# A two-layer decoder trunk: table loads moved ahead of stores, gate stores in quarters, and the dots of a V slot moved ahead of its split

## The chip, the cores and the metric

The kernel runs on one core of a Trainium2 chip. The metric is the device time of one execution in microseconds. The median of three timed runs before the change is 3729.75 us (3727.84 to 3729.91).

## The reference, cut to what matters

The reference is one inference step of a two-layer decoder. After a mixer each layer has an expert-retrieval block, and the change touches only this block:

```python
def _peer(x, wq, keys, u_tab, v_tab):
    q = (xf @ wq).reshape(n, PEER_HEADS, 2, PEER_DK // 2)
    s = jnp.einsum('nhpd,hpkd->nhpk', q, keys)
    ...                                   # top 16 of 128, twice; top 16 of the 256 sums: experts, gate
    def one(args):
        xi, ei, gi = args
        hi = jax.nn.gelu(jnp.einsum('bed,bd->be', jnp.take(u_tab, ei, axis=0), xi))
        return jnp.einsum('be,bed->bd', gi * hi, jnp.take(v_tab, ei, axis=0))
```

There are 520 tokens, 8 heads of 16 experts each, and two tables of 16,384 rows of 1024 numbers in each layer.

## The kernel before

**Two ways for the tokens.** For 392 tokens the whole tables are multiplied on TensorE ("dense"). The other 128 tokens gather their 128 rows of each table by indirect DMA on GpSimd, and VectorE takes the products ("dots", 256 a layer: 128 with U, 128 with V).

**Stage U.** The table U comes in 128 chunks of 512 KB. Chunk c goes through a ring of RING = 4 places: SyncE (SP) loads it into `wraw` (`load_chunk`, L509), ScalarE rounds it to `whi` (`round_chunk`, L673), VectorE writes the rest to `wlo` (`split_chunk`, L941), TensorE multiplies it in 24 matmuls (`first_table`, L1626), and ScalarE takes the product through a gelu into `hid` (`take_hidden`, L806). SP then stores `hid` to DRAM (`store_h`, L535). The first eight chunks are mixed with 16 chunks of the query weights (`mixed`, L104). The ring is closed by semaphores: a load of chunk s+4 waits for `w_lo` of chunk s, and the rounding of chunk s+4 waits until TensorE is done with chunk s.

**Gates.** From chunk 28 on, TensorE also builds the dense gate matrix, 98 groups of four tokens (`gate_group`, L1659), one group behind each chunk up to chunk 115 and two behind each of 116 to 120. VectorE and ScalarE write the one-hot operands `oh` of a group one chunk ahead (`one_hots`). ScalarE copies the result to `gst` (`take_gates`, L854). Seven groups make a block of 1792 KB; `gst` holds two blocks, and SP stores a block to DRAM in one DMA (`store_gates`, L540), two chunks after its last group. `take_gates` waits at the first group of a block until the block two before it has been stored.

**The loop on SP** (L558 to L565), one step for each chunk, in this order: `load_next(slot)`, which issues the load four chunks on, then `store_h` of the chunk in this slot, which waits until ScalarE has taken it, then a gate store if one is due. SP runs its program in order, so a load stands behind the store of the chunk before.

**VectorE in U**, one step for each chunk from 8 on (L1217 to L1224): split, one-hots, a part of the ranking of experts (`RANK_BY`), then dots of the sparse tokens, which begin at chunk 77: 105 dots before stage U ends. ScalarE in U, in order: take the product, round the chunk four on, one-hots, take the gates.

**Stage V.** The gates come back from DRAM (`gc`), also the hidden values (`hl`); VectorE multiplies them to `wt` (`gated`), ScalarE rounds that to `wth`, VectorE writes the rest to `wtl` (`split_wt`), and TensorE multiplies with the 128 chunks of V, 24 matmuls each (`second_table`, L1701). VectorE's step c is written out at L1246 to L1252: `gated(c + 3)`, `split_wt(c + 2)`, `split_next` (the split of the chunk four on), `dots(N_U + c)`. Every fifth step has two dots, the others one. ScalarE's step c (L912 to L916): round `wt` of c+3, then round the chunk c+4, which waits until TensorE is done with chunk c.

**Gathers.** GpSimd fills five row buffers; the gather of dot n waits until dot n-5 is done (L645).

Of the kernel before, what the change touches and what calls it, by code (L numbers as in the profile page):

```python
# [30 lines left out]
P = 128  # L31
# [30 lines left out]
BLOCK = SPAN_T // SUB  # L62
NB = ND // SPAN_T
# [12 lines left out]
N_AB, N_WO, N_WQ, N_U, N_INC = 24, 8, 16, 128, 16  # L76
# [3 lines left out]
C_MIX = [C_WO0 + N_WO, 0]  # L80
# [23 lines left out]
def mixed(slot):  # L104

    if slot >= N_MIX:
        return "u", slot - N_WQ
    return ("u", slot // 3) if slot % 3 == 2 else ("q", slot // 3 * 2 + slot % 3)


def groups_by(c):

    return min(N_GROUPS, max(0, min(c, G_TWO) - G_ONE) + 2 * max(0, min(c, G_END) - G_TWO))


def group_slot(n):

    return next(c for c in range(N_U) if groups_by(c + 1) > n)


LOOK = 1
CHUNK_NS, GROUP_NS, SPLIT_NS, HOTS_NS, DOT_NS = 4300, 890, 1300, 1550, 1250
RANK_NS = [1900] + [480] * 4 + [650] * 4 + [630] * 4 + [480] * 4 + [650] * 3 + [4400] + [2350] * 6 + [1300]
EXP_PART = 20
# [2 lines left out]
def plan():  # L127
# [5 lines left out]
    for c in range(MIXED, N_U):  # L133
        hots = groups_by(c + 1 + LOOK) - groups_by(c + LOOK)
        room += CHUNK_NS + GROUP_NS * (groups_by(c + 1) - groups_by(c)) - SPLIT_NS - HOTS_NS * hots
# [109 lines left out]
def trunk(nc, i, o):  # L245
    with ExitStack() as ctx:
# [94 lines left out]
        gst = place("gst", [P, 2, P, SPAN_T], F32)  # L341
# [23 lines left out]
        gates = [nc.dram_tensor(f"gates{n}", (NB, P, P, SPAN_T), F32, kind="Internal").ap() for n in range(DEPTH)]  # L365
# [6 lines left out]
        def sem(name):  # L372
            return ctx.enter_context(nc.semaphore(name))
# [16 lines left out]
        gates_out = [sem(f"gates_out{n}") for n in range(2)]  # L390
# [113 lines left out]
        @block.sync  # L504
        def _(e):
            for dst, src in ((xt[:], i["xt"]), (wf[:], i["wf"]), (vec[:], i["vec"]), (cst[:], i["cst"])):
                e.dma_start(dst, src).then_inc(setup_in, 16)

            def load_chunk(s, src):  # L509

                if s >= RING:
                    e.wait_ge(w_lo, s - RING + 1)
                e.dma_start(wraw[:, s % RING, :], src).then_inc(w_in[s % RING], 16)

            def chunk_source(s):

                for layer in range(DEPTH):
                    if C_V[layer] <= s < C_V[layer] + N_U:
                        at = (layer * N_U + s - C_V[layer]) * P
                        return i["v"][at:at + P, :]  # L520
                    if C_MIX[layer] <= s < C_V[layer]:
                        kind, n = mixed(s - C_MIX[layer])
                        if kind == "u":
                            return i["u"][layer * N_U + n].rearrange("p k c -> p (k c)")
                        s = C_MIX[layer] + n
                        break
                return i["w"][s - (2 * N_U if s > C_V[0] else 0)].rearrange("p k c -> p (k c)")

            def load_next(s):
                if s + RING < N_CHUNKS:  # L530
                    load_chunk(s + RING, chunk_source(s + RING))

            def peer_tables(layer):

                def store_h(c):  # L535

                    e.wait_ge(chunk_taken, taken(C_MIX[layer]) + table_at(c) + 1)
                    e.dma_start(hidden[layer][c], hid[:, c % RING, :]).then_inc(h_out[c % RING], 16)

                def store_gates(b):  # L540

                    e.wait_ge(gate_taken, layer * N_GROUPS + (b + 1) * BLOCK)
                    e.dma_start(gates[layer][b], gst[:, b % 2]).then_inc(gates_out[b % 2], 16)

                def load_h(c):
                    if c >= RING:
                        e.wait_ge(g_used, layer * N_U + c - RING + 1)
                    e.wait_ge(h_out[c % RING], 16 * (layer * N_U // RING + c // RING + 1))
                    e.dma_start(hl[:, c % RING, :], hidden[layer][c]).then_inc(h_in[c % RING], 16)

                def load_gates(g, half):
                    if g >= 2 and half == 0:
                        e.wait_ge(g_used, layer * N_U + CPL * (g - 1))
                    at = slice(half * (NB // 2), (half + 1) * (NB // 2))
                    e.dma_start(gc[:, g % 2, at].rearrange("p b c n -> p b (c n)"),
                                gates[layer][at, :, g * CPL:(g + 1) * CPL, :].rearrange("b p c n -> p b (c n)")).then_inc(g_in[g % 2], 16)

                for slot in range(N_WQ + N_U):  # L558
                    load_next(C_MIX[layer] + slot)
                    kind, c = mixed(slot)  # L560
                    if kind == "u":
                        store_h(c)
                        for b in range(NB):
                            if c == group_slot((b + 1) * BLOCK - 1) + 2:
                                store_gates(b)  # L565
                for par in range(2):
                    e.wait_ge(gates_out[par], 16 * (NB // 2) * (layer + 1))
                load_gates(0, 0)
                load_gates(0, 1)
                for c in range(RING):  # L570
                    load_h(c)
                for c in range(N_U):
                    load_next(C_V[layer] + c)
                    if c + RING < N_U:
                        load_h(c + RING)
                    if c % CPL < 2 and c // CPL + 1 < N_U // CPL:
                        load_gates(c // CPL + 1, c % CPL)

            for s in range(RING):
                load_chunk(s, chunk_source(s))  # L580
            for s in range(N_AB - 2):
                load_next(s)
            e.wait_ge(pages_in, 16)
            e.wait_ge(chunk_done, C_WO0)
            load_cached(e, 0, 0, i["ck"], None)
            load_cache(e, 0)

            e.wait_ge(pv_done, HEADS * QT)
            for s in range(N_AB - 2, C_MIX[0]):
                load_next(s)  # L590
            peer_tables(0)
            for s in range(C_INC, C_MIX[1]):
                load_next(s)
            peer_tables(1)
            for k in range(KB):
                e.wait_ge(ln_out, 8 * 4 + k + 1)
                e.dma_start(o["y"][:, k, :], xt[:, k, :]).then_inc(y_out, 16)
            e.wait_ge(y_out, 16 * KB)
# [73 lines left out]
        def _(e):  # L672
# [123 lines left out]
            def peer(layer):  # L796
# [57 lines left out]
                def take_gates(n):  # L854

                    b = n // BLOCK
                    if n % BLOCK == 0 and (b >= 2 or layer):
                        e.wait_ge(gates_out[b % 2], 16 * (layer * (NB // 2) + b // 2))
                    e.wait_ge(gate_done, layer * N_GROUPS + n + 1)
                    e.activation(gst[:, b % 2, :, n % BLOCK * SUB:(n % BLOCK + 1) * SUB],  # L860
                                 aux[:, n % 2, :].rearrange("p (a n) -> p a n", n=SUB), ACT.Copy).then_inc(gate_taken, 1)
# [18 lines left out]
                for slot in range(N_WQ + N_U):  # L880
                    kind, n = mixed(slot)
# [14 lines left out]
                    if kind == "u":  # L896
                        for g in range(groups_by(n + LOOK), groups_by(n + 1 + LOOK)):
                            one_hots(g)
# [39 lines left out]
        def _(e):  # L938
# [7 lines left out]
            def split_next(s):  # L946
                if s + RING < N_CHUNKS and not C_AB + N_AB - 2 <= s < C_AB + N_AB:
                    split_chunk(s + RING)
# [207 lines left out]
            def peer(layer):  # L1156
# [37 lines left out]
                def dots(slot):  # L1194

                    for n in range(dots_by(slot - 1), dots_by(slot)):
                        dot(n)
# [19 lines left out]
                for n in range(MIXED, N_U):  # L1217
                    split_next(C_MIX[layer] + table_at(n))
                    for g in range(groups_by(n + LOOK), groups_by(n + 1 + LOOK)):
                        one_hots(g)  # L1220
# [16 lines left out]
                def split_wt(c):  # L1237
                    e.wait_ge(wt_hi, layer * N_U + c + 1)
                    e.tensor_tensor(wtl[:, c % RING, :], wt[:, c % 2, :], wth[:, c % RING, :].bitcast(F32), ALU.subtract).then_inc(wt_lo, 1)  # L1239
# [6 lines left out]
                for c in range(N_U):  # L1246
                    if c + 3 < N_U:
                        gated(c + 3)
                    if c + 2 < N_U:
                        split_wt(c + 2)  # L1250
                    split_next(C_V[layer] + c)
                    dots(N_U + c)  # L1252

                e.wait_ge(dot_done, (layer + 1) * DOTS)
                e.tensor_tensor(ysum[0:ST, 0, :], ysum[0:ST, 0, :], ysum[0:ST, 1, :], ALU.add).then_inc(y_ready, 1)
# [610 lines left out]
```

## Time and profile before

| what | value |
|---|---|
| median of three runs | 3729.75 us |
| profiled execution | 3736.83 us, of it a span of 3734.8 us |
| TensorE busy | 91% of the span |
| VectorE, ScalarE, GpSimd busy | 66%, 39%, 21% |
| moved by DMA | 835 MB, 224 GB/s over the span |

The profiled execution is 7.1 us (0.2%) above the median. Stage U of the first layer lies between 491 and 1333 us of the span, V between 1354 and 1949; in the second layer they lie between 2246 and 3088 and between 3109 and 3703. Matmul records overlap, so TensorE's busy share says little; the distance of one chunk's end to the next is what counts.

### The profile page before, as it was taken

The page shows a single profiled execution, that of the slowest core. Times are in us where ns is not written, and L with a number is a line of the kernel's source. Part 1 is how long each engine was busy: PE and PEld are TensorE (multiplying, and loading weights), DVE is VectorE, ACT ScalarE, POOL GpSimd, SP SyncE. Part 2 cuts the span into 40 slices and gives each one's busy share as a digit, 9 for nine tenths or more (in the row PEclk, how much of TensorE's full clock was granted, in tenths as well). Part 3 has the DMA queues.
Part 4 walks back from the last instruction along what each step waited for, and adds up shares of the span by engine and source line. Part 5 has one row for each costly group of instructions (what it writes and reads, how often), then busy time and mean ns, then how long its engine had stood idle before and what let it go on. Part 6 is the DMA issues. An engine that isn't in the chain of part 4 may idle for free.

```text
span 3734.8 us, 54628 instructions
## 1 busy us (share of the span) xinstructions
PE 3397.7 (91%) x19630; PEld 3154.9 (84%) x19630; DVE 2474.6 (66%) x5134; ACT 1444.4 (39%) x2581; POOL 767.2 (21%) x690
## 2 busy tenths in 40 slices
PE   8998999999988979999988889999998897999998
PEld 8833789999988969998988789999888887989897
DVE  3243379777666767777773348876776666777777
ACT  3222143455545523333323223345554552333333
POOL 3211010000143332222221000000023333222221
PEclk9898999999999989999999789999999998999999
DMA  4354313454688899999971112355468889999994
GB/s 138 118 150 124 127 68 110 157 187 164 219 306 303 282 370 331 339 325 337 324 266 59 35 51 90 123 176 182 158 241 297 298 315 351 341 325 340 323 337 160
DMA packets 315827, 835.34 MB, mean 224 GB/s; under 512 B 32249, under 2 KB 155257, under 8 KB 311441
## 3 DMA queue, kind: packets, MB, share of 16 engines
q1 hardware_dynamic: 233472, 541.63, 42.6%
q0 software_dynamic: 82192, 291.85, 22.3%
q8 instruction: 66, 1.08, 0.1%
q14 instruction: 97, 0.79, 0.1%
HBM read 726.25 MB, written 107.11 MB: 223 GB/s over the span
## 4 chain that ended last, share of the span: by engine, by line
PE 51%; DVE 17%; DMA 11%; issue 10%; ACT 10%; SPq 1%; DVEq 0%; ACTq 0%; POOLq 0%; POOL 0%
PE pstr L1632 20%; PE pstr L1421 13%; DMA wraw<-in_u 8%; DVE ysum L1192 8%; ACT whi L678 7%; PE aux L1667 4%; DVE wt L1233 3%; PE aux L1709 2%; PE pstr L1709 2%; PE pstr L1543 2%; PE pstr L1563 1%; DVE wlo L944 1%; DVE rows L1179 1%; DMA wraw<-in_v 1%; PE aux L1452 1%
## 5 line engine op out<-in xcount | busy, mean ns | idle before, releaser
L944 DVE TENSOR_TENSOR wlo<-wraw,whi 128x1024 fp32r<-128x1024 f32 x600 | 733.8, 1224 | 868.4 <-ACT whi L678 867.7
L678 ACT ACTIVATE whi<-wraw 128x1024 fp32r<-128x1024 f32 x600 | 629.3, 1050 | 341.0 <-DMA wraw<-in_u 212.6
L1632 PE MATMUL pstr<-xh,whi 128*128 128x392 f32 x2048 | 734.5, 359 | 5.3 <-ACT hid L812 5.3
L1632 PE MATMUL pstr<-xl,whi 128*128 128x392 f32 x2048 | 711.3, 347 | 0.0
L1632 PE MATMUL pstr<-xh,wlo 128*128 128x392 f32 x2048 | 709.0, 346 | 0.0
L651 POOL DMA_INDIRECT rows<-in_ur,idx x256 | 343.8, 1343 | 1532.0 <-DVE hs L1179 962.3
L1709 PE MATMUL aux<-wth,whi 128*128 128x392 f32 x1024 | 373.1, 364 | 97.9 <-DVE wtl L1239 97.1
L908 ACT ACTIVATE wth<-wt 128x392 fp32r<-128x392 f32 x256 | 136.1, 532 | 823.4 <-DVE wt L1233 823.4
L651 POOL DMA_INDIRECT rows<-in_v,idx x256 | 290.7, 1136 | 712.3 <-DVE ysum L1192 627.0
L1632 PEld LDWEIGHTS pstr<-xh,whi 128*128 128x128 f32 x2048 | 398.3, 194 | 6.0 <-issue 5.9
L1632 PEld LDWEIGHTS pstr<-xl,whi 128*128 128x128 f32 x2048 | 397.1, 194 | 0.0
L1632 PEld LDWEIGHTS pstr<-xh,wlo 128*128 128x128 f32 x2048 | 395.7, 193 | 0.0
L1709 PE MATMUL aux<-wth,wlo 128*128 128x392 f32 x1024 | 351.1, 343 | 0.0
L1709 PE MATMUL pstr<-wth,wlo 128*128 128x392 f32 x1024 | 350.1, 342 | 0.0
L1709 PE MATMUL aux<-wtl,whi 128*128 128x392 f32 x1024 | 350.1, 342 | 0.0
L1709 PE MATMUL pstr<-wtl,whi 128*128 128x392 f32 x1024 | 348.7, 341 | 0.0
L1709 PE MATMUL pstr<-wth,whi 128*128 128x392 f32 x1024 | 347.6, 340 | 0.0
L1667 PE MATMUL aux<-oh,oh 128*128 128x128 f32 x1568 | 227.3, 293 | 115.1 <-DVE oh L1212 114.6
L1667 PEld LDWEIGHTS aux<-oh,oh 128*128 128x128 f32 x1568 | 213.3, 204 | 131.7 <-issue 67.2
L1709 PEld LDWEIGHTS aux<-wth,whi 128*128 128x128 f32 x1024 | 193.0, 188 | 150.0 <-DVE wtl L1239 97.4
L1421 PE MATMUL pstr<-xh,whi 128*128 128x260 f32 x1408 | 295.4, 291 | 26.1 <-DVE xl L959 25.8
L1192 DVE SCALAR_TENSOR_TENSOR ysum<-rows,hs,ysum 128x1024 f32<-128x1024 f32 x252 | 318.7, 1278 | 0.5
(240 smaller groups left out, 5405.9 us busy)
## 6 DMA issues: line engine op xcount, KB each, us to landing
wraw<-in_u SPq DMA_DIRECT2D x256, 512.0 KB, 4.4
wraw<-in_v SPq DMA_DIRECT2D x256, 512.0 KB, 4.9
hidden<-hid SPq DMA_DIRECT2D x256, 196.0 KB, 1.9
gates<-gst SPq DMA_DIRECT2D x28, 1792.0 KB, 8.6
gc<-gates SPq DMA_DIRECT2D x64, 784.0 KB, 8.6
hl<-hidden SPq DMA_DIRECT2D x256, 196.0 KB, 5.3
wraw<-in_w SPq DMA_DIRECT2D x88, 512.0 KB, 3.5
kv<-in_ck SPq DMA_DIRECT2D x32, 256.0 KB, 3.2
```

Of the source, the lines that this page charges most:

```text
L651: e.indirect_dma_start(rows[0:ST, n % BUFS, :], None, table, bass.IndirectOffsetOnAxis(ap=idx[0:ST, j:j + 1], axis=0)).then_inc(rows_in[n ...
L678: e.activation(whi[:, s % RING, :], wraw[:, s % RING, :], ACT.Copy).then_inc(w_hi, 1)
L908: e.activation(wth[:, c % RING, :], wt[:, c % 2, :], ACT.Copy).then_inc(wt_hi, 1)
L944: e.tensor_tensor(wlo[:, s % RING, :], wraw[:, s % RING, :], whi[:, s % RING, :].bitcast(F32), ALU.subtract).then_inc(w_lo, 1)
L1179: e.tensor_tensor_reduce(data, data, xrow[0:ST, :], 1.0, 0.0, ALU.mult, ALU.add, hs[0:ST, 0, j:j + 1]).then_inc(dot_done, 1)
L1192: e.scalar_tensor_tensor(y, data, w, y, ALU.mult, ALU.add).then_inc(dot_done, 1)
L1233: e.tensor_tensor(wt[:, n % 2, :].rearrange("p (b n) -> p b n", n=SPAN_T), hl[:, n % RING, :].rearrange("p (b n) -> p b n", n=SPAN_T), gc[ ...
L1421: mm = e.matmul(pstr[:, r % 2, h, 0:HALF], w[:, r, k * P:(k + 1) * P], x[:, k, h * HALF:(h + 1) * HALF], start=k == 0 and w is whi and x i ...
L1543: mm = e.matmul(cached[0:BH, half, :].rearrange("p (g c) -> p g c", g=4), qd[:, b, k, :], pages[:, :, k * P:(k + 1) * P], start=False, sto ...
L1632: mm = e.matmul(pstr[:, r % 2, 0, 0:ND], w[:, r, k * P:(k + 1) * P], x[:, k, 0:ND], start=k == 0 and w is whi and x is xh, stop=k == KB - ...
L1667: mm = e.matmul(out[:, :, r], oh2[:, slot, r, :], oh1[:, slot, r, :], start=True, stop=True)
L1709: mm = e.matmul(bank(d)[:, 0:ND], w[:, r, d * P:(d + 1) * P], x[:, r, :], start=first and w is whi and x is wth, stop=last and w is wlo)
```

## The change

It does three things. First, the loop on SP runs three steps longer, and the stores in a step belong to the slot three before it: the load of chunk s+4 is now issued after the store of chunk s-4 and not after that of chunk s-1. Second, a gate block leaves in four DMAs of 448 KB, each with a quarter of `gst`'s middle axis; the first leaves with the store of the chunk after the block's last group, the others with the three stores that follow. The semaphore counts go up by the factor PIECES. Third, in VectorE's step of stage V the dots stand ahead of the split.

```diff
+BEHIND, PIECES = 3, 4
...
-                def store_gates(b):
+                def store_gates(b, part):
 
                     e.wait_ge(gate_taken, layer * N_GROUPS + (b + 1) * BLOCK)
-                    e.dma_start(gates[layer][b], gst[:, b % 2]).then_inc(gates_out[b % 2], 16)
+                    at = slice(part * (P // PIECES), (part + 1) * (P // PIECES))
+                    e.dma_start(gates[layer][b][:, at, :], gst[:, b % 2, at, :]).then_inc(gates_out[b % 2], 16)
...
-                for slot in range(N_WQ + N_U):
-                    load_next(C_MIX[layer] + slot)
-                    kind, c = mixed(slot)
+                for slot in range(N_WQ + N_U + BEHIND):
+                    if slot < N_WQ + N_U:
+                        load_next(C_MIX[layer] + slot)
+                    kind, c = mixed(slot - BEHIND) if slot >= BEHIND else ("q", 0)
                     if kind == "u":
                         store_h(c)
                         for b in range(NB):
-                            if c == group_slot((b + 1) * BLOCK - 1) + 2:
-                                store_gates(b)
+                            for part in range(PIECES):
+                                if c == min(group_slot((b + 1) * BLOCK - 1) + 1 + part, N_U - 1):
+                                    store_gates(b, part)
                 for par in range(2):
-                    e.wait_ge(gates_out[par], 16 * (NB // 2) * (layer + 1))
+                    e.wait_ge(gates_out[par], 16 * PIECES * (NB // 2) * (layer + 1))
...
-                        e.wait_ge(gates_out[b % 2], 16 * (layer * (NB // 2) + b // 2))
+                        e.wait_ge(gates_out[b % 2], 16 * PIECES * (layer * (NB // 2) + b // 2))
...
                         split_wt(c + 2)
+                    dots(N_U + c)
                     split_next(C_V[layer] + c)
-                    dots(N_U + c)
```

SP around the first gate block of the first layer, before: a load (`wraw`), the store of the chunk in the same slot (`hidden`), and the whole block behind the store of one chunk.

```order
L513 DMA wraw<-in_u 128x1024
L538 DMA hidden<-hid 128x392
L513 DMA wraw<-in_u 128x1024
L538 DMA hidden<-hid 128x392
L543 DMA gates<-gst 128x3584
L513 DMA wraw<-in_u 128x1024
L538 DMA hidden<-hid 128x392
L513 DMA wraw<-in_u 128x1024
```

The same place on SP now; a `hidden` row belongs to the chunk three before the one whose slot it stands in.

```order
L514 DMA wraw<-in_u 128x1024
L539 DMA hidden<-hid 128x392
L545 DMA gates<-gst 128x896
L514 DMA wraw<-in_u 128x1024
L539 DMA hidden<-hid 128x392
L545 DMA gates<-gst 128x896
L514 DMA wraw<-in_u 128x1024
L539 DMA hidden<-hid 128x392
L545 DMA gates<-gst 128x896
L514 DMA wraw<-in_u 128x1024
L539 DMA hidden<-hid 128x392
L545 DMA gates<-gst 128x896
```

What moved: the gate block is in four pieces with a load between each two, and every load stands three stores nearer to the program's start.

VectorE early in stage V of the first layer, before: `wlo` is the split, the two L1179 rows are one dot.

```order
L1233 TENSOR_TENSOR wt<-hl,gc 128x392
L1239 TENSOR_TENSOR wtl<-wt,wth 128x392
L944 TENSOR_TENSOR wlo<-wraw,whi 128x1024
L1179 ISA rows,hs<-rows,xrow 128x1024
L1179 ISA hs 128x1
L1233 TENSOR_TENSOR wt<-hl,gc 128x392
```

The same place on VectorE now.

```order
L1237 TENSOR_TENSOR wt<-hl,gc 128x392
L1243 TENSOR_TENSOR wtl<-wt,wth 128x392
L1183 ISA rows,hs<-rows,xrow 128x1024
L1183 ISA hs 128x1
L948 TENSOR_TENSOR wlo<-wraw,whi 128x1024
L1237 TENSOR_TENSOR wt<-hl,gc 128x392
```

What moved: the dot stood between the split and the next chunk's `wt`, and now stands ahead of the split, so that `wt` of the next chunk follows the split at once.

## Rows read from the trace of the kernel before

**Rows 1.** Timeline by engine around a gate store (start us, us, instruction, [idle <-releaser]):

```profile
891.84 0.43 SPq L543 DMA_DIRECT2D gates<-gst  x1
892.31 0.46 SPq L513 DMA_DIRECT2D wraw<-in_u  x1
...
900.01 1.06 ACT L678 ACTIVATE whi<-wraw 128x1024 fp32r<-128x1024 f32 x1 [3.38 <-DMA wraw<-in_u]
...
903.75 1.84 PE L1667 MATMUL aux<-oh,oh 128*128 128x128 f32 x8 [2.48 <-DVE oh L1212]
906.63 0.74 PE L1656 MATMUL aux<-cst,dense_pick 96*128 96x96 f32 x3 [1.04 <-DVE dense_pick L1378]
```

**Rows 2.** Chain of waits, pieces in order of time (start us, us, what):

```profile
629.10 25.76 PE pstr L1632 x144
...
729.73 0.89 PE aux L1667 x8
```

**Rows 3.** Timeline of SP: stores of chunks 28, 77, 116 and 127, first layer:

```profile
723.01 0.33 SPq L538 DMA_DIRECT2D hidden<-hid  x1
...
1012.54 0.32 SPq L538 DMA_DIRECT2D hidden<-hid  x1
...
1269.49 0.32 SPq L538 DMA_DIRECT2D hidden<-hid  x1
...
1333.21 0.32 SPq L538 DMA_DIRECT2D hidden<-hid  x1
```

**Rows 4.** Stretches: length, busy of PE, PEld, DVE, ACT, POOL; PEclk, DMA share, GB/s:

```profile
490.00:630.00 140.00, 140.00 (x1088) 139.91 (x1086) 118.56 (x612) 48.85 (x82) 1.81 (x2) 1.00 0.26 92
723.00:1012.50 289.50, 268.23 (x1574) 263.93 (x1574) 205.70 (x484) 167.35 (x355) 15.34 (x11) 0.96 0.53 179
1012.50:1269.50 257.00, 220.21 (x1258) 216.11 (x1259) 175.32 (x306) 128.91 (x284) 102.07 (x73) 0.93 0.86 304
1269.50:1354.50 85.00, 57.35 (x340) 56.75 (x339) 55.32 (x92) 33.91 (x69) 33.99 (x26) 0.86 0.90 336
1354.50:1900.00 545.50, 523.76 (x2821) 500.23 (x2822) 416.89 (x519) 172.60 (x235) 154.43 (x137) 1.00 0.95 332
```

**Rows 5.** Waits, 720 to 1355 us, PE (for whom: us, times, longest):

```profile
PE aux L1667 <- DVE oh L1212: 57.4, 21, 6.2
```

**Rows 6.** Waits of SP's queue, 630 to 1310 us:

```profile
SPq L538 <- ACT hid L812: 566.7, 116, 9.8
SPq L513 <- DVE wlo L944: 1.7, 1, 1.7
```

**Rows 7.** DMA issues of the whole span: KB each, median us to landing:

```profile
wraw<-in_u SPq DMA_DIRECT2D x256, 512.0 KB, 4.4
gates<-gst SPq DMA_DIRECT2D x28, 1792.0 KB, 8.6
rows<-in_ur,idx POOLq DMA_INDIRECT x256, 6.9
```

**Rows 8.** Timeline of ACT and DVE over one slot of stage V:

```profile
1365.11 1.04 ACT L678 ACTIVATE whi<-wraw 128x1024 fp32r<-128x1024 f32 x1
...
1366.18 1.23 DVE L944 TENSOR_TENSOR wlo<-wraw,whi 128x1024 fp32r<-128x1024 f32 x1 [1.07 <-ACT whi L678]
1367.33 1.22 DVE L1179 CUSTOM_DVE_ANT_0 rows<-rows,xrow 128x1024 f32<-128x1024 f32 x1
...
1368.47 0.56 DVE L1233 TENSOR_TENSOR wt<-hl,gc 128x392 f32<-128x392 f32 x1
...
1369.07 0.53 ACT L908 ACTIVATE wth<-wt 128x392 fp32r<-128x392 f32 x1 [2.92 <-DVE wt L1233]
1369.51 1.05 ACT L678 ACTIVATE whi<-wraw 128x1024 fp32r<-128x1024 f32 x1
```

**Rows 9.** Timeline of PE: first and last matmul of stage V, first layer:

```profile
1354.49 0.66 PE L1709 MATMUL aux<-wth,whi 128*128 128x392 f32 x1 [25.07 <-DVE wtl L1239]
...
1948.69 0.34 PE L1709 MATMUL pstr<-wth,wlo 128*128 128x392 f32 x1
```

**Rows 10.** DMA queues from 1300 to 1345 us, total:

```profile
DMA packets 5946, 17.17 MB, mean 382 GB/s; under 512 B 543, under 2 KB 2697, under 8 KB 5816
```

## The prediction

> **What bounds the kernel now.** I read first the stretches with the granted clock and the DMA share [rows 4], then who waits for whom [rows 5, 6], and then one slot each of U and V in the timeline [rows 1, 8]. In the undisturbed head of U, 490 to 630 us, TensorE runs without a gap at clock 1.00. From chunk 28 on it is below that: 0.96, then 0.93, then 0.86 [rows 4]. What TensorE can do at best: 144 matmuls, six chunks, take 25.76 us, so 4.29 us a chunk; a gate group adds 0.89 [rows 2]. A slot of U with a group is 5.18 us.
>
> The place where it falls behind is the gate store [rows 1]. At 891.84 SP issues 1792 KB, and the load behind it, issued at 892.31, lands only when ScalarE has waited 3.38 us for it (900.01). ScalarE's rounding is late, so VectorE's split and the one-hots behind it are late, and TensorE waits 2.48 us for `oh` before a gate group. The cause is SP's order: it stands 566.7 us waiting for a chunk to be taken, and only 1.7 us for the ring place itself [rows 6]. The load of chunk s+4 goes out when chunk s-1 has been taken, one slot before ScalarE wants to round it: 5.2 us against a median landing of 4.4 [rows 7]. Anything on the queues makes it late. TensorE's waits for `oh` from chunk 28 to V are 57.4 us in 21 pieces [rows 5], and behind each wait come matmuls at the lower of its two clock levels.
>
> Stage V is held by a loop through two engines, not by TensorE. In one slot [rows 8]: ScalarE rounds a chunk (1365.11), VectorE splits it (1366.18), does a dot (1367.33), makes the next `wt` (1368.47), ScalarE rounds that (1369.07) and is free for the next chunk at 1369.51. That is 4.40 us with one dot, and 1.15 more (from one VectorE start to the next) with two. 101 slots of 4.40, 25 of 5.55 and two without a dot of 3.25 give 590 us; V takes 594.5, from 1354.49 to 1949.0 [rows 9]. TensorE alone would need 128 x 4.29 = 549.5.
>
> **Loads ahead of stores, early U** (chunks 28 to 77). The load of chunk s+4 now stands behind the store of chunk s-4 instead of s-1. Its own wait, for the split of chunk s, is over about 2.7 us after TensorE ends chunk s-4 (rounding and split are 1.07 and 1.15 from start to start [rows 8]; 0.5 for taking the product is an estimate). It is wanted at the end of chunk s: four slots of 5.18 less 2.7, so 18 us against a landing of 4.4, or 4.4 + 8.6 = 13 behind a whole gate store [rows 7]. It is covered twice. The stretch takes 289.5 us for 49 slots [rows 3]; at 5.18 they are 253.8, and 35.7 are lost. I leave 4.5 as an estimate for what the load does not cause, the turns of picks, where TensorE waits for `dense_pick` (1.04 and a 0.74 operation at chunk 60 [rows 1]) and the start of the groups. **Gain 31 us a layer**, from 26 (twice as much stays) to 35.
>
> **Gate stores in quarters.** They add 42 DMA issues a layer at 0.43 us on SP [rows 1], which has 567 us of waiting to hide them in: nothing. Of a piece's landing there is no row; by the nearest ones it lies between 4.4 us (a 512 KB load) and 8.6 (the whole block) [rows 7]. The last piece leaves with the chunk four after the block's last group, and ScalarE writes that half of `gst` again at the eighth: three slots, 15.5 us, so even 8.6 costs nothing.
>
> **Late U and the handover** (chunk 77 to the first matmul of V), 1012.54 to 1354.49, 342 us [rows 3, 9]. Here the gathers run too, and there are two bounds. TensorE's: 39 slots of 5.18, five with two groups of 6.07, six of 4.29 are 258; the handover, 21.3 us now (1333.21 to 1354.49), must still bring the first gates and hidden values, 8.6 us for as many bytes as a gate store and two or so for the `wt` chain, up to the whole 21.3: I take 15, sum 273. DMA's: 304 x 257 + 336 x 85 = 106.7 MB [rows 4]. At the share of 0.86 they go at 304, so at a share of 1 at 353 GB/s: 302 us. Against that stands one stretch in which the queues were full and moved 382 GB/s [rows 10]: 279 us. I take the middle of 273 and 302, **288: gain 54**, from 40 to 69.
>
> The Trainium skill (DMA: Bandwidth & Descriptors, Where 436 GB/s comes from) says that for transfers between HBM and SBUF the HBM side binds at about 358 GB/s. By that the stretch would take 298 us, and V would come to 551; the 382 GB/s of [rows 10] speak against it as a ceiling.
>
> **Dots ahead of the split in V.** Nothing is added. The loop through ScalarE loses the dot [rows 8]: rounding to split 1.07, split 1.15, `wt` to `wth` 0.60, `wth` to the next rounding 0.44, in all 3.26 us, under 4.29. VectorE's own work in a slot with two dots is 1.15 for the split, 0.5 each for `wt` and `wtl`, 2.3 for the dots, 4.45 in all; it ends 0.2 late, and the next slot, with one dot, has 1.0 spare. The split now stands behind the dots, so a late gather would delay it; but the chunk split is needed three slots later. So TensorE is next: 549.5. DMA: 332 x 594.5 = 197.4 MB, at 332/0.95 = 349 GB/s [rows 4] 565 us; at 382 below TensorE. I take **557: gain 37.5**, from 29.5 to 45.
>
> **Sum.** 31 + 54 + 37.5 = 122.5 a layer. The second layer runs the same code; 245 in all. Against the profiled execution, 3736.8: 3492. The median of the runs is 7.1 lower: **3485 us**. All three terms at TensorE's bound: 35 of which I allow 31, 69, 45, so 290 and 3440. All at DMA's share of 1: 31 + 40 + 29.5, so 201 and 3529.
>
> **Rivals.** (1) DMA at its ceiling in late U and V: 3529, just worked out. For it: shares of 0.86 and 0.95 [rows 4] that must rise by a tenth. Against: 382 GB/s.
> (2) The gathers are crowded out by loads that are no longer held back, and the dots hold VectorE. Five buffers and two dots a slot: five dots need an issue of 1.4 us on GpSimd (102.07 us for 73 [rows 4]), a landing L and a dot of 1.2, against 2.5 slots, 12.95 us. From L = 10.4 on it decides; the median is 6.9 [rows 7]. At L = 12 a slot is 5.84; the 105 dots of U fill 52 slots, which cost 34 us, so late U takes 307: gain 35, sum 207, 3523. The same mechanism **makes the kernel slower** when those 52 slots lose, over TensorE's 273, what the stretch and the two other terms give, 342 - 273 + 68.5 = 137 us: a slot of 7.8, five dots in 19.5, L above 16.9; at L = 18 a slot is 8.24, late U 432, and the time about 3773.
> (3) Only U gains; in V the dots wait for rows and hold the split as long as they held `wt`. 85 a layer: 3560. Against: 1.2 dots in a slot and five buffers leave 18 us for a landing.
> (4) The change does not do what it says: the load stays late, since `w_lo` takes the place of the store as SP's wait. 1.7 us in [rows 6] speaks against it. Time as before, 3730.
>
> **How the numbers follow.** Forecast 0.62; (1) 0.17; (2) still faster 0.08, slower 0.04; (3) 0.05; (4) 0.04. Low end 3440, TensorE's bound everywhere; high end 3580, which takes in (1), (3) and (2) up to a landing of 13. A measurement of this kernel tells 0.2% from no change: faster 0.92, same 0.04, slower 0.04.
>
> **What the changed profile would show.** Right: the wait of ScalarE's rounding for `wraw<-in_u` nearly gone, TensorE's 57.4 us for `oh` down to some 5, stores of chunks 5.18 us apart around the gate stores, SP still waiting for `hid`; in V, slots of 4.29 to 4.35 also where there are two dots, clock 1.00, V near 557. Wrong: VectorE waiting for `rows` in late U (rival 2) or ahead of the split in V (3); landings of loads over 8 us at a DMA share of 1.0 with slots over 5.18 (1). If the granted clock falls under 1.00 in a gapless stretch, TensorE's bound itself is wrong.

## The result, and the profile after

| | before | changed |
|---|---|---|
| median of the timed runs | 3729.83 us | 3464.13 us |
| lowest to highest | 3727.84 to 3733.97 | 3461.83 to 3465.40 |
| ratio, 95% interval | | 0.9286 (0.9270 to 0.9302) |
| span of the profiled execution | 3734.8 us | 3463.3 us |

The kernel is 7.1% faster, 266 us. The forecast was 3485 us within 3440 to 3580.

The stretches of the changed kernel, from the store of chunk 28 on: early U, late U, the end of U with the handover, and V of the first layer; the last row is V of the second. The columns are those of [rows 4].

```profile
720.00:978.00 258.00, 256.10 (x1581) 255.05 (x1582) 207.60 (x486) 166.38 (x356) 17.17 (x12) 1.00 0.59 202
978.00:1180.30 202.30, 202.30 (x1254) 202.30 (x1253) 174.16 (x303) 127.03 (x283) 111.73 (x73) 1.00 1.00 379
1180.30:1259.70 79.40, 55.58 (x340) 55.25 (x338) 55.42 (x91) 33.70 (x69) 34.09 (x26) 0.87 0.96 362
1259.70:1811.00 551.30, 551.27 (x3072) 551.09 (x3072) 454.15 (x562) 201.99 (x255) 208.92 (x146) 1.00 0.97 351
2881.00:3432.00 551.00, 551.00 (x3073) 550.96 (x3072) 454.81 (x567) 198.79 (x252) 208.91 (x146) 1.00 0.95 345
```

Late U is now gapless: 202.3 us of TensorE in 202.3, where [rows 4] has 220 in 257, and the granted clock is 1.00 and not 0.93 there. V is gapless too. Early U is down from 289.5 to 258. Only the third row, the handover, has a gap: TensorE is busy 55.6 of 79.4 us, and the stretch is hardly shorter than its 85 us before.

TensorE's waits from 640 to 1330 us of the changed kernel (for whom: us, times, longest) answer to [rows 5]:

```profile
PE aux L1713 <- DVE wtl L1243: 23.9, 1, 23.9
PE aux L1660 <- DVE dense_pick L1382: 3.4, 2, 2.4
PE aux L1671 <- DVE oh L1216: 1.3, 1, 1.3
```

The 57.4 us for one-hots are 1.3. What is left is one wait of 23.9 us, the handover, and the turns of picks. SP's own waits from 630 to 1240 us answer to [rows 6]:

```profile
SPq L539 <- ACT hid L816: 287.6, 115, 4.2
SPq L514 <- DVE wlo L948: 210.9, 117, 6.2
```

The ring place is now a wait of SP in its own right: a load goes out as soon as its place is free.

One slot of V in the changed kernel, ScalarE and VectorE, answers to [rows 8]:

```profile
1317.47 1.06 ACT L682 ACTIVATE whi<-wraw 128x1024 fp32r<-128x1024 f32 x1 [0.91 <-PE pstr L1713]
...
1318.56 1.23 DVE L948 TENSOR_TENSOR wlo<-wraw,whi 128x1024 fp32r<-128x1024 f32 x1 [0.89 <-ACT whi L682]
1319.70 0.56 DVE L1237 TENSOR_TENSOR wt<-hl,gc 128x392 f32<-128x392 f32 x1
1320.18 0.56 DVE L1243 TENSOR_TENSOR wtl<-wt,wth 128x392 fp32r<-128x392 f32 x1
1320.66 1.28 DVE L1196 SCALAR_TENSOR_TENSOR ysum<-rows,hs,ysum 128x1024 f32<-128x1024 f32 x1
1322.85 1.23 DVE L948 TENSOR_TENSOR wlo<-wraw,whi 128x1024 fp32r<-128x1024 f32 x1 [0.92 <-ACT whi L682]
```

From split to split it is 4.29 us, TensorE's time for a chunk, and ScalarE's rounding waits for TensorE (0.91): both engines have time to spare. In [rows 8] the dot stood between split and `wt`, and nothing waited for TensorE.

**Where the time came from.** For each kernel of this study the table gives, for both layers, the time from the store of chunk 28 to those of 77, 116 and 124 (SP's timeline), from there to the first matmul of V, and from that to the end of its last (TensorE's timeline).

| kernel | 28 to 77 | 77 to 116 | 116 to 124 | 124 to V | V | median, us |
|---|---|---|---|---|---|---|
| before | 289.5, 287.8 | 257.0, 258.3 | 49.4, 49.6 | 35.6, 35.5 | 594.5, 594.4 | 3729.8 |
| changed | 257.8, 258.0 | 202.3, 202.3 | 43.8, 43.6 | 35.6, 36.1 | 551.4, 551.6 | 3464.1 |
| loads only | 257.8, 258.0 | 202.5, 202.4 | 43.9, 43.2 | 35.9, 35.9 | 594.2, 595.8 | 3553.2 |
| quarters only | 260.4, 262.3 | 236.9, 235.8 | 51.0, 54.1 | 34.2, 34.2 | 595.2, 595.2 | 3648.3 |
| dots only | 289.0, 287.3 | 257.8, 249.6 | 50.1, 50.1 | 35.3, 35.3 | 551.1, 551.3 | 3646.5 |
| whole gates | 257.8, 258.0 | 202.3, 202.4 | 43.3, 43.5 | 36.2, 36.8 | 551.5, 552.0 | 3464.4 |
| one behind | 257.8, 258.0 | 206.7, 205.7 | 45.2, 47.4 | 37.5, 37.0 | 552.4, 551.9 | 3479.1 |
| four buffers | 257.8, 258.0 | 202.5, 202.5 | 49.4, 47.2 | 28.0, 29.6 | 551.8, 552.1 | 3457.3 |
| three buffers | 257.8, 258.0 | 234.1, 234.9 | 52.2, 52.4 | 35.1, 36.0 | 552.1, 552.3 | 3542.8 |
| more traffic | 257.8, 258.0 | 202.3, 202.3 | 43.6, 44.0 | 36.1, 35.8 | 622.0, 622.1 | 3608.7 |
| last blocks at once | 257.8, 258.0 | 202.3, 202.3 | 44.8, 45.6 | 33.7, 32.9 | 551.6, 551.4 | 3461.6 |
| hidden first | 257.8, 258.0 | 202.3, 202.3 | 44.0, 44.1 | 35.6, 37.0 | 551.3, 552.5 | 3464.9 |
| fewer early dots | 257.8, 258.0 | 202.3, 202.3 | 43.2, 43.2 | 22.8, 23.2 | 551.5, 552.2 | 3436.9 |
| all three | 257.8, 258.0 | 202.6, 202.3 | 43.2, 43.2 | 22.8, 23.2 | 551.1, 551.4 | 3441.0 |

In the first layer the change takes 31.7 us from early U, 60.3 from chunk 77 to V, and 43.1 from V. The ratios given below are to the kernel before as it was timed beside each run, 3731.3 to 3734.5 us in the median.

### The profile page after: what moved, and what is told of

It is laid out like the page before. It is cut to its first block, busy times and chain, and to the rows that moved or that the text cites. A ratio compares the mean times of both kernels' runs of the same rounds, so it can differ in the third digit from the quotient of the medians.

```text
span 3463.3 us, 54712 instructions
## 1 busy us (share of the span) xinstructions
PE 3294.0 (95%) x19630; PEld 3119.8 (90%) x19630; DVE 2474.0 (71%) x5134; ACT 1463.8 (42%) x2581; POOL 875.9 (25%) x690
## 3 DMA queue, kind: packets, MB, share of 16 engines
q0 software_dynamic: 82192, 291.85, 23.2%
## 4 chain that ended last, share of the span: by engine, by line
PE 90%; DVE 3%; DMA 3%; ACT 2%; issue 1%; POOL 0%; SPq 0%; POOLq 0%; ACTq 0%; DVEq 0%
PE pstr L1636 29%; PE aux L1713 16%; PE pstr L1713 16%; PE pstr L1425 14%; PE aux L1671 5%; PE pstr L1547 2%; PE pstr L1567 2%; PE aux L1456 1%; PE aux L1465 1%; DMA gates<-gst 1%; PE aux L1626 1%; PE pstr L1520 1%; PE aux L1767 1%; PE aux L1766 1%; DMA rows<-in_ur,idx 1%
## 5 line engine op out<-in xcount | busy, mean ns | idle before, releaser
L1636 PE MATMUL pstr<-xh,whi 128*128 128x392 f32 x2048 | 719.2, 351 | 0.0
L1636 PE MATMUL pstr<-xl,whi 128*128 128x392 f32 x2048 | 698.2, 341 | 0.0
L1636 PE MATMUL pstr<-xh,wlo 128*128 128x392 f32 x2048 | 697.2, 340 | 0.0
L655 POOL DMA_INDIRECT rows<-in_ur,idx x256 | 364.4, 1423 | 1308.2 <-DVE hs L1183 755.4
L655 POOL DMA_INDIRECT rows<-in_v,idx x256 | 378.1, 1477 | 550.1 <-DVE ysum L1196 461.3
L1713 PE MATMUL aux<-wth,whi 128*128 128x392 f32 x1024 | 351.1, 343 | 48.0 <-DVE wtl L1243 48.0
L1636 PEld LDWEIGHTS pstr<-xh,whi 128*128 128x128 f32 x2048 | 385.9, 188 | 0.1
L816 ACT ACTIVATE hid<-pstr 128x392 f32<-128x392 f32 x256 | 127.3, 497 | 533.9 <-PE pstr L1636 533.7
L1183 DVE CUSTOM_DVE_ANT_0 rows<-rows,xrow 128x1024 f32<-128x1024 f32 x256 | 305.7, 1221 | 17.6 <-DMA rows<-in_ur,idx 17.2
L1425 PE MATMUL pstr<-xh,wlo 128*128 128x260 f32 x1408 | 287.3, 286 | 0.0
```

The source lines that it names most:

```text
L655: e.indirect_dma_start(rows[0:ST, n % BUFS, :], None, table, bass.IndirectOffsetOnAxis(ap=idx[0:ST, j:j + 1], axis=0)).then_inc(rows_in[n ...
L816: e.activation(hid[:, c % RING, :], pstr[:, s % 2, 0, 0:ND], ACT.Gelu_apprx_tanh).then_inc(chunk_taken, 1)
L1183: e.tensor_tensor_reduce(data, data, xrow[0:ST, :], 1.0, 0.0, ALU.mult, ALU.add, hs[0:ST, 0, j:j + 1]).then_inc(dot_done, 1)
L1425: mm = e.matmul(pstr[:, r % 2, h, 0:HALF], w[:, r, k * P:(k + 1) * P], x[:, k, h * HALF:(h + 1) * HALF], start=k == 0 and w is whi and x i ...
L1636: mm = e.matmul(pstr[:, r % 2, 0, 0:ND], w[:, r, k * P:(k + 1) * P], x[:, k, 0:ND], start=k == 0 and w is whi and x is xh, stop=k == KB - ...
L1713: mm = e.matmul(bank(d)[:, 0:ND], w[:, r, d * P:(d + 1) * P], x[:, r, :], start=first and w is whi and x is wth, stop=last and w is wlo)
```

## The experiments

### Which of the three parts does it

**Loads only.** The changed kernel, with a gate block in one store as before and V as before:

```diff
-BEHIND, PIECES = 3, 4
+BEHIND, PIECES = 3, 1
...
-                                if c == min(group_slot((b + 1) * BLOCK - 1) + 1 + part, N_U - 1):
+                                if c == group_slot((b + 1) * BLOCK - 1) + 2:
...
-                    dots(N_U + c)
                     split_next(C_V[layer] + c)
+                    dots(N_U + c)
```

> Loads ahead of the stores by three slots, but a gate block in one store two chunks after its last group, and V's slot as before. Theory (the load's lead of one slot was the whole loss in U; quarters are only politeness): U gains what it gains with all three parts, 92 us a layer (early U 31.7, chunk 77 to V 60.3), V stays at 594 us: about 3546 us. Rival (the size of the gate store is the cause, and lead alone leaves the collision): half of the gain in U or less, 3635 us or more, with ScalarE's rounding still waiting for the load behind a gate store.

3553.2 us, ratio 0.9516 (0.9500 to 0.9532): 7 us over the theory, far under the rival. In U the stretches are those of the changed kernel to 0.6 us, with whole gate stores. TensorE's waits for one-hots, 640 to 1240 us:

```profile
PE aux L1671 <- DVE oh L1216: 1.3, 1, 1.3
```

The lead of the loads is enough for the whole gain in U.

**Quarters only.** BEHIND = 0 and V as before:

```diff
-BEHIND, PIECES = 3, 4
+BEHIND, PIECES = 0, 4
```

> Gate blocks in quarters over four chunks, but loads where they were, behind the store of the chunk before, and V's slot as before. Theory: the lead of 5.2 us stays; a quarter ahead of a load adds about 1.2 us to a landing of 4.4, so early U loses little, but in late U, where gathers share the queues, loads stay late: a gain of 20 in early U and 10 in late U a layer, about 3670 us. Rival (size of the store is the cause): all of U's gain, 3546 us.

3648.3 us, ratio 0.9751 (0.9720 to 0.9781): 85 us, more than the theory gave it and far less than the rival. Early U comes almost to TensorE's bound (260.4 against 257.8): there a quarter ahead of a load does not make it late enough to reach TensorE. Late U stays 34 us above. Waits of this kernel from 720 to 1300 us:

```profile
ACT whi L682 <- DMA wraw<-in_u: 78.8, 40, 8.2
PE aux L1671 <- DVE oh L1216: 27.2, 18, 3.8
```

So in early U it took both, the short lead and the whole store, to make TensorE wait: either part of the change alone removes nearly all of the loss. In late U, with gathers on the queues, a lead of one slot is too short even with quarters.

**Dots only.** The kernel before with the two lines of V exchanged:

```diff
-                    split_next(C_V[layer] + c)
                     dots(N_U + c)
+                    split_next(C_V[layer] + c)
```

> Only the dots of a V slot ahead of the split; stage U as before. Theory (V was held by the loop through ScalarE and VectorE with the dot in it): V goes from 594 to 551 us in each layer, U stays: about 3643 us. Rival (V was fed better only because U left its queues in another state, or DMA is V's bound): 3700 us or more.

3646.5 us, ratio 0.9774 (0.9746 to 0.9801). V is 551 us in both layers. U is as before in the first layer; in the second, late U is 8.7 us shorter (249.6 for 258.3), which nothing here explains. The waits in the first layer's U, 640 to 1300 us:

```profile
ACT whi L678 <- DMA wraw<-in_u: 90.2, 32, 7.3
PE aux L1667 <- DVE oh L1212: 58.7, 22, 6.3
```

The two gains add up within the noise: 180 us for the loads and 87 for the dots make 267, and the change gives 266; each of them is known to some 6 to 10 us.

**Whole gates.** All of the change but the quarters:

```diff
-BEHIND, PIECES = 3, 4
+BEHIND, PIECES = 3, 1
...
-                                if c == min(group_slot((b + 1) * BLOCK - 1) + 1 + part, N_U - 1):
+                                if c == group_slot((b + 1) * BLOCK - 1) + 2:
```

> All of the change but the quarters: a gate block leaves in one store two chunks after its last group. Theory: a load has 18 us of lead, and a whole store adds 8 to 10 us to its landing, so nothing waits: 3464 us, within 8. Rival (in late U, where a load lands in 7.5 us even with quarters, lead and whole store together are not enough): 3490 to 3520 us, with waits of ScalarE for loads two chunks after each block.

3464.4 us, ratio 0.9279 (0.9263 to 0.9294). Beside early loads the quarters neither help nor harm.

### How much lead is needed

```diff
-BEHIND, PIECES = 3, 4
+BEHIND, PIECES = 1, 4
```

> The change with BEHIND = 1 in place of 3: a load is one slot earlier than before the change, not three. Theory: the lead is then two slots, 10.4 us, against a landing of 7.5 us in late U with quarters: nearly all of the gain, 3464 to 3475 us. Rival (loads must be three slots early because their landing swings, up to 12 us near the end of U): 3500 us or more, with ScalarE waiting for loads in late U.

3479.1 us, ratio 0.9323 (0.9304 to 0.9341): 15 us above the change, between the two expectations. Early U needs no more than one step. Late U loses 4 us a layer and the end of U some more. Waits of this kernel, 970 to 1250 us:

```profile
ACT whi L682 <- DMA wraw<-in_u: 16.8, 11, 4.2
ACT whi L682 <- DMA wraw<-in_v: 10.0, 2, 5.2
```

From 1000 to 1180 us its loads land in 8.5 us in the median, under the lead of two slots, 10.4 us, but some come later; a median alone does not size a lead.

### Do the gathers pace VectorE

**Four buffers, three buffers.** One line each:

```diff
-BUFS = 5
+BUFS = 4
```

> The change with four row buffers for the gathers in place of five. This prices the rival that gathers hold VectorE. By its formula four dots need 1.4 + 8.4 (landing now) + 1.2 = 11.0 us against two slots of 5.18 = 10.4: a slot of 5.5 in late U, 17 us a layer: about 3498 us, with VectorE waiting for rows. If gathers are far from pacing: 3464 us.

3457.3 us, ratio 0.9269 (0.9249 to 0.9290). No loss in late U; 7 us lower than the change, but with intervals that overlap. The end of U (116 to 124) is longer by 5.6 and 3.6 us, and the handover (124 to V: 28.0 and 29.6) shorter by 7.6 and 6.5. That the handover has less in front of it with at most four gathers under way is a reading that this run does not test: with three buffers it is as long as in the change.

```diff
-BUFS = 5
+BUFS = 3
```

> The change with three row buffers. By the same formula three dots need 9.5 (landing 6.9) to 11.0 us (8.4) for one and a half slots: a slot of 6.3 to 7.3 in late U, 60 to 112 us a layer; in V three dots have two and a half slots, 10.7 us, and are just in time: 3584 to 3688 us. If gathers don't pace late U at all: under 3500 us. With dots ahead of the split, a late row must now also show as a late split.

3542.8 us, ratio 0.9494 (0.9470 to 0.9518), between the two expectations. Late U takes 234.1 us for 39 slots, 6.00 each. VectorE's waits, first from 960 to 1300 us (late U), then from 1300 to 1860 (V):

```profile
DVE rows L1183 <- DMA rows<-in_ur,idx: 83.2, 66, 4.7
```

```profile
DVE ysum L1196 <- DMA rows<-in_v,idx: 32.3, 19, 4.1
```

The gathers do pace VectorE if there are three buffers, so the rival was real as a mechanism. But its formula counted the issue on GpSimd twice: in the trace the time to landing starts with the issue. Three dots then take the landing and one dot, 8.0 (the median of late U) + 1.2 = 9.2 us for one and a half slots, a slot of 6.1 where 6.00 were measured; with the issue added once more it would be 7.1. Four take 8.3 + 1.2 = 9.5 for two slots of 5.18, so four buffers suffice in late U, as they did. With five buffers the landing may grow to 12.95 - 1.2 = 11.7 us; in the changed kernel it is 8.4 in late U. In V the waits for rows stand ahead of the split and still cost nothing (552 us), as the prediction had argued: the chunk split there is needed three slots later.

### Where DMA's ceiling is

Two more stores of 196 KB in every slot of V:

```diff
                     load_next(C_V[layer] + c)
+                    for copy in range(2):
+                        e.dma_start(spare[layer][c, copy], hid[:, c % RING, :]).then_inc(spare_out, 16)
...
+                e.wait_ge(spare_out, 16 * 2 * N_U * (layer + 1))
```

> The change with two more stores of 196 KB from SBUF to DRAM in every slot of V, which nobody waits for before the end of the stage. It measures DMA's ceiling: V then moves 1.54 + 0.40 MB a slot, 249 MB a layer. If the ceiling is 410 GB/s, V takes 606 us a layer and the kernel 3574; at 382 GB/s 651 and 3664; at 353, the figure from the busy share, 704 and 3770. If there is no ceiling that V can reach, 3464.

3608.7 us, ratio 0.9676 (0.9655 to 0.9698). V takes 622 us; its stretch in the first layer, and what ScalarE waits for in it:

```profile
1260.00:1880.00 620.00, 573.04 (x3062) 563.67 (x3060) 452.38 (x557) 197.29 (x254) 217.80 (x146) 0.96 1.03 392
...
ACT whi L687 <- DMA wraw<-in_v: 121.4, 56, 5.9
```

V now waits for its loads, so about 392 GB/s is the ceiling for this mix, V's traffic with the two stores, between the expected cases. The change runs V at 351 and late U at 379 (first fence): under it, but not by much. The share of busy time had said otherwise: [rows 4] has 304 GB/s at a share of 0.86, and the same stretch now moves 379 at 1.00, not 353.

### What holds the handover

The chain of waits of the changed kernel at the end of U (start us, us, what):

```profile
1211.43 9.88 DMA rows<-in_ur,idx
...
1225.29 15.64 DMA gates<-gst
...
1242.07 15.69 DMA hl<-hidden
```

and its DMA from 1200 to 1255 us (KB each, median us to landing):

```profile
DMA packets 7993, 20.97 MB, mean 381 GB/s; under 512 B 708, under 2 KB 3583, under 8 KB 7990
...
gates<-gst SPq DMA_DIRECT2D x6, 448.0 KB, 10.9
...
gc<-gates SPq DMA_DIRECT2D x2, 784.0 KB, 12.9
hl<-hidden SPq DMA_DIRECT2D x4, 196.0 KB, 11.6
...
rows<-in_ur,idx POOLq DMA_INDIRECT x22, 8.3
```

The last quarter of the last block, which the change sends later than before, is a link of the chain. Two theories: the order of stores and loads holds the handover, or the bytes in front of it, 22 gathers of 512 KB above all. VectorE's own work, the last dots of U, does not hold it: before the first `wt` of V it waits for the hidden values (waits of the changed kernel from 640 to 1330 us).

```profile
DVE wt L1237 <- DMA hl<-hidden: 10.2, 1, 10.2
```

**Order: the last two blocks at once, then also the hidden values first.**

```diff
-                                if c == min(group_slot((b + 1) * BLOCK - 1) + 1 + part, N_U - 1):
+                                if c == group_slot((b + 1) * BLOCK - 1) + 1 + (part if b < NB - 2 else 0):
```

> The change, but the last two gate blocks of a layer leave with all four quarters at once, in the chunk after their last group. In the changed kernel the last quarter is issued at 1225.29 us and lands at 1240.99, 4.6 us after the last product is stored, and SP waits for it before it loads the first gates of V. Theory (that wait is on the path): up to 4.6 us a layer, 3455 us. Rival (the queues are full there, 381 GB/s from 1200 to 1255 us, so only the bytes count): 3464 us.

3461.6 us, ratio 0.9276 (0.9260 to 0.9292): not to be told from the change. In the first layer the last gate store now lands 13.3 us before the store of chunk 127, in place of 4.5 behind it, and V still begins 22.4 us behind that store, in place of 23.3.

```diff
+                for c in range(RING):
+                    load_h(c)
                 for par in range(2):
                     e.wait_ge(gates_out[par], 16 * PIECES * (NB // 2) * (layer + 1))
                 load_gates(0, 0)
                 load_gates(0, 1)
-                for c in range(RING):
-                    load_h(c)
```

> The kernel of the run before, and SP issues the first four loads of hidden values ahead of the wait for the gate stores and of the first loads of gates; they were 11.6 us from issue to landing and the last that VectorE waited for. Theory: the handover then ends with the gates, 12.9 us after the last gate store at the latest and sooner with less in front of them: 3 to 8 us a layer more, 3440 to 3450 us. Rival (bytes alone count): 3464 us.

3464.9 us, ratio 0.9286 (0.9268 to 0.9305): nothing. Counted from the store of chunk 127, the four hidden values are there after 10.5 us in place of 22.8, but the second half of the first gates after 21.5 in place of 20.8. Neither order takes more than 1.2 us off the handover.

**Bytes: fewer early dots.**

```diff
+EARLIEST = 84
...
-            while room >= DOT_NS and dotted < DOTS // 2:
+            while room >= DOT_NS and dotted < EARLIEST:
```

> The change, with 84 dots of U done before stage U ends in place of 105; the 21 others move into V, whose slots then have 1.37 dots in the mean. Theory (the handover from U to V is held by bytes: 24 gathers stand in U's last twelve slots, in which the queues are full): 21 gathers of 512 KB less before the first gates are loaded, 11 MB at 390 GB/s, of which at most the 10 us above TensorE's bound in the handover can come back: 5 to 10 us a layer, 3445 to 3455 us; V stays at 551, since its rate rises from 350 to 370 GB/s, under the 390 that the run with more traffic showed. Rival (the handover is held by the order of its loads, or V is pushed over DMA's ceiling): 3464 us or more.

3436.9 us, ratio 0.9207 (0.9194 to 0.9219): 27 us under the change and clear of its interval, more than expected. Its DMA from 1180 to 1246 us, the end of U and the handover:

```profile
gates<-gst SPq DMA_DIRECT2D x8, 448.0 KB, 4.0
...
gc<-gates SPq DMA_DIRECT2D x2, 784.0 KB, 5.6
hl<-hidden SPq DMA_DIRECT2D x4, 196.0 KB, 6.2
rows<-in_ur,idx POOLq DMA_INDIRECT x6, 6.7
```

With six gathers there, gates and hidden values land in half the time, and from the store of chunk 124 to V it is 22.8 us in place of 35.6 (from that of chunk 127, 9.9 in place of 23.3). V pays nothing, although it now moves 376 GB/s:

```profile
1250.00:1790.00 540.00, 540.00 (x3014) 540.00 (x3014) 470.10 (x599) 199.52 (x253) 276.99 (x167) 1.00 1.01 376
```

**All three: 84 early dots, four buffers, the last blocks at once.**

```diff
-BUFS = 5
+BUFS = 4
...
+EARLIEST = 84
...
-            while room >= DOT_NS and dotted < DOTS // 2:
+            while room >= DOT_NS and dotted < EARLIEST:
...
-                                if c == min(group_slot((b + 1) * BLOCK - 1) + 1 + part, N_U - 1):
+                                if c == group_slot((b + 1) * BLOCK - 1) + 1 + (part if b < NB - 2 else 0):
```

> 84 early dots, four row buffers and the last two gate blocks at once, together. Four buffers alone took 7 us off, the last blocks at once nothing clear. Theory: the three take bytes from the same place, so they do not add: 3440 to 3450 us. Rival (each acts on its own): 3435 us or less.

3441.0 us, ratio 0.9219 (0.9206 to 0.9232), the same as with fewer early dots alone within the noise. The gains do not add, which fits the theory that all three act on the same bytes.

## Why the prediction was right, point by point

**Loads ahead of stores, early U: right.** 31 us were forecast and 31.7 measured; "loads only" gives it alone. What was left for picks and the first groups, 4.5 us, is there, as 4.0: 257.8 against 253.8. One reading of the trace before was too wide: not behind each of TensorE's 21 waits for `oh` does the clock stand at its lower level. The granted clock goes to 0.50 at 12 of them and stays at 1.00 at the other nine. No term of the sum rests on it.

**Quarters: right that they cost nothing, and incomplete.** Beside early loads they bring nothing either ("whole gates"); alone they would have brought 85 us, a route to half of U's gain that the prediction did not weigh. The bound on a piece's landing was wrong: 8.4 us in the median of late U and up to 10.4, and up to 17.0 at the end of U, where 4.4 to 8.6 were given; late U now moves 379 GB/s, where [rows 4] has 304. No wait of ScalarE for it shows: in late U the margin of three slots, 15.5 us, held, and the half that is stored last, with the 17.0, is not written again in that layer.

**Late U and the handover: right in the sum, wrong in its two halves.** 288 us were forecast and 281.7 measured (978.0 to 1259.7). The step that failed is the extrapolation of the DMA share to 353 GB/s, which pulled the term up from TensorE's bound: late U moves 379 and runs at TensorE's bound (202.3 us for 202.0). In the other direction the handover, 21.3 us before from the store of chunk 127 to V, was taken as 15 and did not shrink: it is 23.3, and TensorE's wait in it 23.9 us, 25.07 before [rows 9]. Full queues set it, as "fewer early dots" shows; neither of the two orders tried takes more than 1.2 us off it. The two errors were about 15 and 8 us and worked against each other, so that the sum came within 6 us is luck in part.

The Trainium skill (DMA: Bandwidth & Descriptors, Where 436 GB/s comes from) gives about 358 GB/s as what binds between HBM and SBUF, and works it out as half of what a stack of HBM gives to two cores. For this kernel, which runs on one core, the traces do not agree: 379 GB/s over 202 us in the changed kernel and 392 over 620 in "more traffic".

**Dots ahead of the split: right, undersized.** 37.5 us were forecast and 43.1 measured; V is 551.4 us, TensorE's 549.5 and little else. Again the DMA share had pulled the middle up. "Dots only" shows that U has no part in it, and "three buffers" that a row late by up to 4.1 us ahead of the split does not reach TensorE.

**The sum.** The span is 271.5 us shorter, and 245 were forecast. Of the 26.5 between, V has 10.9 and the late stretch 13.7 over both layers (the second layer's goes from 343.4 to 282.0); early U is even. The median is only 21 us under the forecast, because the profiled execution before lay 7 us above its median and the one after 1.

**The rivals.** DMA at its ceiling: the ceiling exists, at 392 GB/s, but above what the change needs. Gathers: the mechanism is real and takes hold with three buffers, not with four, but the price counted the issue twice, so the point from which it decides is a landing of 11.7 us, not 10.4. Only U gains: no. The load stays late because the ring place takes over as the wait: SP does wait 210.9 us for the ring place now, but early enough that TensorE never sees it.

## What to carry to other kernels

Where one queue issues loads and stores in program order, a store that waits for a result also holds back every load behind it: put each store as many steps later as the load's ring allows, and size that lead by the slow landings, not by the median. In a loop through two engines, work that neither of them is waiting for belongs in the place where the engine waits anyway, here ahead of the split and not between the split and what the other engine needs next. Once steady stages run at the bound of one engine, look at the stage boundary: there, taking bytes away (21 dots moved to a stage with room) helped, and the two reorderings tried did not.

## What the runs showed of the hardware that was not expected

The busy share of the DMA engines was no measure of what rate was left: 304 GB/s at 0.86, 379 at 1.00, 392 at 1.03 in three stretches with 512 KB loads, gathers and stores. At the end of U, with the queues full (381 GB/s from 1200 to 1255 us in the first layer), 448 KB stores took up to 15.6 us to land, and up to 17.0 in the second layer; before the change a whole block of four times the size took between 6.9 and 10.5. And the landing time of an indirect DMA, as the trace counts it, includes its issue on GpSimd: with three buffers a slot took 6.00 us, and 8.0 + 1.2 over one and a half slots gives 6.1.
